# When a chunk's first factor quad is made: three queues of a two-layer float32 block reordered

## The reference

```
def sq_relu_mlp(xn, w_in, w_out):
    h = jax.nn.relu(xn @ w_in)
    return (h * h) @ w_out
...
        h = h + sq_relu_mlp(rms_norm_2(h, norm_mlp_g[i]), mlp_w_in[i], mlp_w_out[i])
```

## Time and profile before

| what | value |
| --- | --- |
| median of 3 runs | 1724.16 us |
| profiled execution, time | 1724.16 us |
| its span in the trace | 1722.1 us |
| PE busy | 1711.2 us (99%) |
| DVE busy | 1018.0 us (59%) |
| ACT busy | 844.4 us (49%) |
| POOL busy | 962.9 us (56%) |

### The profile page before, as it was taken

One profiled execution on the slowest core, in us unless ns is written; L12 is line 12 of the kernel. 1 busy time (PEld: TensorE's weight loads), 2 busy tenths in 40 slices (PEclk: granted clock), 3 DMA queues, 4 the chain that ended last, 5 costly groups with the idle time before them and its releaser, 6 DMA issues.

```text
span 1722.1 us, 26916 instructions
## 1 busy us (share of the span) xinstructions
PE 1711.2 (99%) x9185; PEld 1434.9 (83%) x9185; DVE 1018.0 (59%) x1977; ACT 844.4 (49%) x1434; POOL 962.9 (56%) x1107
## 2 busy tenths in 40 slices
PE   9999999999999999999999999999999999999998
PEld 7778888888888778888989898877777889898987
DVE  6875755555211455568757674567777675757543
ACT  5665555555322444435444443446565454535443
POOL 6443655555555434356666657655554665666674
PEclk9999999999999999999999999999999999999999
DMA  5221333333334222223333323423331243333232
GB/s 189 77 68 62 98 98 97 97 97 94 101 98 141 95 68 83 74 86 111 98 110 96 101 86 94 133 84 105 106 105 59 86 135 99 98 99 98 74 98 98
DMA packets 48655, 167.82 MB, mean 97 GB/s; under 512 B 5376, under 2 KB 6672, under 8 KB 48528
## 3 DMA queue, kind: packets, MB, share of 16 engines
q1 hardware_dynamic: 48272, 166.05, 30.2%
q10 hardware_dynamic: 288, 0.52, 0.1%
HBM read 164.31 MB, written 2.24 MB: 97 GB/s over the span
## 4 chain that ended last, share of the span: by engine, by line
PE 93%; DVE 4%; ACT 1%; issue 1%; DMA 0%; POOL 0%; SPq 0%; DVEq 0%; ACTq 0%
PE bank L735 18%; PE bank L638 7%; PE bank L643 7%; PE bank L637 7%; PE bank L1032 5%; PE bank L1033 5%; PE bank L1037 5%; PE bank L1441 5%; PE bank L1442 4%; PE bank L1450 4%; PE bank L753 3%; PE bank L759 3%; PE bank L754 3%; PE bank L1080 2%; PE bank L1085 2%; PE bank L1079 2%
## 5 line engine op out<-in xcount | busy, mean ns | idle before, releaser
L501 POOL TENSOR_TENSOR w_lo<-stage,w_hi 128x256 fp32r<-128x256 f32 x936 | 742.2, 825 | 599.3 <-ACT w_hi L1503 335.1
L1503 ACT ACTIVATE w_hi<-stage 128x1024 fp32r<-128x1024 f32 x234 | 246.6, 1054 | 257.6 <-PE bank L638 96.6
L638 PE MATMUL bank<-xn_lo,w_hi 128*128 128x512 f32 x544 | 211.9, 390 | 0.0
L637 PE MATMUL bank<-xn_hi,w_hi 128*128 128x512 f32 x544 | 211.8, 389 | 0.0
L735 PE MATMUL bank<-xn_hi,w_hi 128*128 128x512 f32 x464 | 189.0, 407 | 0.0
L735 PE MATMUL bank<-xn_lo,w_hi 128*128 128x512 f32 x464 | 182.0, 392 | 0.0
L1032 PE MATMUL bank<-xn_hi,w_hi 128*128 128x512 f32 x352 | 137.1, 389 | 0.0
L1033 PE MATMUL bank<-xn_lo,w_hi 128*128 128x512 f32 x352 | 137.1, 389 | 0.0
L643 PE MATMUL bank<-xn_hi,w_lo 128*128 128x512 f32 x544 | 135.0, 389 | 0.0
L735 PE MATMUL bank<-xn_hi,w_lo 128*128 128x512 f32 x464 | 123.9, 399 | 0.0
L2897 DVE TENSOR_TENSOR x<-x,bank 128x256 f32<-128x256 f32 (+1 forms) x168 | 75.7, 457 | 75.5 <-PE bank L1450 73.4
(11 more groups left out here) (389 smaller groups left out, 3683.8 us busy)
## 6 DMA issues: line engine op xcount, KB each, us to landing
stage<-weights SPq DMA_DIRECT2D x235, 512.0 KB, 3.5
prob<-pairs SPq DMA_DIRECT2D x24, 512.0 KB, 3.9
stage<-pairs SPq DMA_DIRECT2D x24, 512.0 KB, 3.5
bias<-table SPq DMA_DIRECT2D x11, 896.0 KB, 5.4
out<-z SPq DMA_DIRECT2D x8, 256.0 KB, 2.1
x<-x_in SPq DMA_DIRECT2D x3, 512.0 KB, 7.5
bias<-swa_table SPq DMA_DIRECT2D x4, 256.0 KB, 3.7
con<-consts SPq DMA_DIRECT2D x1, 640.0 KB, 9.4
```

What stands on the lines that cost most here:

```text
L501: ins = nc.gpsimd.tensor_tensor(w_lo[:, p_, ks], stage[:, p_, ks], w_hi[:, p_, ks].bitcast(F32), ALU.subtract)
L637: pe.matmul(G[p_][:], w_hi[:, p_, k], hi[:, k], start=(first and k == ks[0]), stop=False)
L638: mm = pe.matmul(G[p_][:], w_hi[:, p_, k], lo[:, k], start=False, stop=False)
L1503: act.activation(w_hi[:, p_], stage[:, p_], ACT.Copy).then_inc(hi_ready, 1)
```

## The change

Three places are edited. POOL's queue takes the low part of A12 directly behind that of A11, and so ahead of the split of tile 5. ACT's queue makes the highs of S1 and A12 of quad j = 0 behind tile 3, where S2's stands already. DVE's queue in `fast_down` has for j = 0 the order that it has for the other quads: the adds of A12 and S2 come later, between and behind the sums and the low part of S1 of the next quad.

```
@@ mlp2_splits, POOL
                     split_los(t, t + 4)
                     split_lo((t + 4) // 2, 0)
-                    quad_lows(q, (HI_A11,))
+                    quad_lows(q, (HI_A11, HI_A12))
                     split_lo((t + 4) // 2, 1)
-                    quad_lows(q, (HI_A12,))
                     split_lo((t + 6) // 2, 0)
@@ mlp2, ACT
                         if e == 2:
                             quad_copy(q)
                             quad_high(q, HI_A11)
+                        elif e == 3:
                             quad_high(q, HI_S1)
                             quad_high(q, HI_A12)
-                        elif e == 3:
                             quad_high(q, HI_S2)
@@ fast, DVE
                     if j:
                         add_product(v, HI_S1)
-                    if j == 0:
-                        add_product(v, HI_A12)
-                        add_product(v, HI_S2)
                     if more:
                         quad_sum(v + 1, 1)
                         quad_sum(v + 1, 2)
-                    if j:
-                        add_product(v, HI_A12)
+                    add_product(v, HI_A12)
                     if more:
                         quad_sum(v + 1, 3)
                         quad_low(v + 1, HI_S1)
-                    if j:
-                        add_product(v, HI_S2)
+                    add_product(v, HI_S2)
```

## The result

The changed kernel takes 1740.94 us (median of 5 runs, 1740.74 to 1742.37), against 1724.16 us of the kernel before on the same chip (5 runs, 1724.09 to 1724.33). The ratio is 1.0098, 95% interval 1.0085 to 1.0111: slower by 16.8 us, where 17 were forecast. The span of the profiled execution went from 1722.1 to 1739.1 us.

The account below looks back on a forecast made before the run. PE, busy 99% of the span, bounds the kernel. Per chunk 1.2 us at tile 5, less 0.27 back, plus 1.9 at S3, taken as 2.85; 6 x 2.85 = 17.1 on 1724.16 gives 1741, range 1735 to 1747.

Parts of the forecast that it names:

- Part 1: POOL's split of tile 5, queued behind the late low of A12, ends late; PE stands 1.2 us in each chunk.
- the chain beside POOL: DVE's first subtraction of tile 3 to ACT's last copy: 2.33 us with POOL splitting beside it, 1.25 with POOL idle.
- Rival 1: Tile 3's chain stays slow (2.33) or the split runs slowest: 4.0 us per chunk, 24 us, 1748; chance 0.12.
- rule of exclusion: A two-SBUF-input DVE operation and a GpSimd operation reading SBUF exclude each other for a whole instruction; without POOL, 1.25 us.
- Part 2: In quad j = 0 the add of S2 comes 2.69 us of instructions later; PE's S3 starts 2.0 us later.
- Rivals 2 and 3: 2: tile 5's split is in time, 1736, chance 0.10; 3: S3 isn't late, 1730, chance 0.06.
- How the two add: Not simply: DVE's end moves 0.85 us, S3 starts 2.85 us later per chunk, 17.1 us over six chunks.
- 0.27 back: PE's old gap in quad j = 0, where it stood for DVE, closes and returns 0.27 us per chunk.
- I count them as nothing: Six of ACT's 24 waits for DVE's sum disappear; not on PE's path, so they were given no gain.
- Rival 4: Not slower: DVE has factors sooner, PE's 0.27 gap closes, margins hold; 1.6 us gained, 1722.5; chance 0.06.
- the other five lie alike: The second chunk's timelines, engine by engine, were taken to stand for the other five fast chunks.

Follow-up runs that it names:

- The doses: Kernel before with the adds of A12 and S2 of quad j = 0 moved behind one sum: 1724.16 us; behind sums 1 and 2: 1728.61 us.

## Why the prediction was right

- **What bounds the kernel.** PE at 99%: right. The time moved by PE's stalls and gaps, 17.2 us in the six chunks, less 0.4 in the first 12 us of the program, which the sum doesn't have; the profiled span grew by 17.0 and the median by 16.8. The waits view lists 15.6 us of new waits; it gives less than the times from start to start (0.82 for the stall of 1.12 at tile 5, for example).
- **Part 1.** Forecast: ACT's copy of tile 3 at 893.56; measured 896.14 - 2.56 = 893.58. The choice between the chain beside POOL (2.33) and the one without (1.25) was the one that mattered, and it was 1.25 to the hundredth. Stall 1.2, measured 1.12 in this chunk; in the first chunk of each layer it was 0.2 to 0.3 longer. Rival 1 needed the slow chain and fell; the run with the POOL and ACT parts (1729.6) shows the size by itself. That the rule of exclusion ("SBUF — State Buffer" in the Trainium skill, "SBUF: two separate sides") gave the 1.25 too is borne out here: 0.42 us each with POOL idle, and 1.48 for one of them, which ended only behind the end of POOL's low beside it.
- **Part 2.** Forecast: the fourth add 2.7 us later, 2.0 per chunk alone. Measured: the add 2.50 us later, 11.6 / 6 = 1.93 per chunk. The doses show that it is this wait. Rivals 2 and 3 each needed one of the stalls to be absent; both are there, six times.
- **How the two add.** DVE's chain behind tile 5 was to move by 0.85; measured 907.80 - 904.33 - 2.56 = 0.91. By pieces: 1.2, 0.27 back, 1.9, together 2.85; measured 1.12, 0.20, 1.86, together 2.78. The gap gave back less because PE came 1.12 - 0.91 = 0.21 later relative to DVE, where the forecast had 0.35.
- **Where it was wrong, without showing in the sum.** "I count them as nothing" was said of ACT's six waits. With the ACT part alone, what moves with them gains 2.5 us: POOL stands idle beside DVE's lows of tile 3, and DVE enters the last tiles without lag. Rival 4 had this mechanism at 1.6 us and at 6 in 100, with ACT's waits as the reason; the mechanism is real, but the lag came from POOL's instructions, and the price is 2.5, because "the other five lie alike" doesn't hold for the gap (0.43 us and not 0.27 in the first chunk of each layer) and the slower start of 0.07 was left out. In the full change the sum isn't missing it: PE stands at tile 5, most of the gap closes by that, and the forecast has this as the 0.27 that comes back. My clock of the combined ACT and DVE parts was also off, 1731.3 for 1732.2.
- **What I said the profile would show** came out but for two things: PE's wait at S3 carries the name of ACT's L2052 and not of DVE's add, and the waits for `w_lo` are listed at 0.8 to 1.1 us, not 1.0 to 1.4. The 0.4 us ahead of the first chunk is a gain outside the six chunks, which I had named as a sign of being wrong; it doesn't bear on the argument, since PE's start in this place differs by up to 0.5 us among the profiles of the other runs too.

## What to carry to other kernels

A move in an in-order queue is priced by what the moved instruction waits for and by what now stands behind it: before moving a producer later, look for a consumer's queue that was just told to take it earlier. Read the margin of each touched release in the timeline (end of the producer against start of the consumer, here 3.2 and 0.76 us); in the runs with moved adds a move cost nothing up to the margin, less the 0.1 us from release to start, and then one for one, times the number of chunks. And on a kernel whose main engine is 99% busy, a wait of another engine that looks free may still be the lag behind a small gap; test each part alone, since the best part of a losing change can be a gain.

## What the runs showed of the hardware

- The name that the profile gives as the releaser of a wait for several semaphores can be wrong for all six places alike: S3's wait is put down to ACT with and without ACT's edit, and the name changes when only DVE's order does. The time between the end of the fourth add and the start of S3 (0.10 us in four profiles) was the better witness.
- DVE's subtractions of 128x256 took 0.42 us with POOL idle; one beside POOL's low of a sub-block took 1.48 us, and the pair of DVE lows that took 3.19 us beside POOL took 0.68 and 0.96 without it. POOL's instructions slow DVE's, which work on other data, enough to decide 2.5 us of the total.
- After a stop of PE in the products, the second matmul started 0.19 us behind the first, where 0.12 is the pace (924.78 behind 924.59 in the changed kernel). So each stop cost 0.07 us more than its length.
